# A decoder's four FFNs on one core: a new order at their seams, and the key/value product moved behind the third FFN's first pair

## Chip, cores and metric

The kernel runs on 1 core of one Trainium2 chip. The metric is the device time of one execution in microseconds, the median of the runs. The host only lays data out.

## What is computed

One inference step of a two-layer decoder on 512 prompt tokens and 64 sample tokens (8 sequences of 8), all in float32. Each layer has an FFN, a mixer and another FFN; the mixer of the first layer is a recurrent block, that of the second is windowed attention. All attention reads one key and value product, computed from the stream x between the second and the third FFN.

```python
def rms_norm(x, g):
    y = x * lax.rsqrt(jnp.mean(x * x, axis=-1, keepdims=True) + EPS)
    return y * g

def swiglu(x, w_gu, w_down):
    gu = x @ w_gu
    return (jax.nn.silu(gu[..., :D_FF]) * gu[..., D_FF:]) @ w_down

for l in range(DEPTH):                                   # DEPTH = 2
    x = x + 0.5 * swiglu(rms_norm(x, ffn1_norm[l]), ffn1_w_gu[l], ffn1_w_down[l])
    hn = rms_norm(x, mix_norm[l])
    x = x + (recurrent_block(hn, ...) if l < N_A else window_attention(hn @ w_q, k, v, ...) @ w_o)
    x = x + 0.5 * swiglu(rms_norm(x, ffn2_norm[l]), ffn2_w_gu[l], ffn2_w_down[l])
    if l == N_A - 1:
        kv = rms_norm(x, kv_norm) @ w_kv                 # 1024 x 256
y = rms_norm(x, final_norm)
```

D_MODEL is 1024 (8 tiles of 128 rows), D_FF 2816 (22 inner tiles).

## The kernel before

Everything is kept transposed: x is 8 tiles of 128 features by 576 tokens, in two halves of 288 columns. Every float32 operand of a matrix product is split into a rounded part (ACT, `_hi`) and a remainder (DVE, `_lo`, line 1266), and each product is three matmuls: high by high, high by low, low by high (`mm_k`, line 529; `product`, line 560).

The kernel is one program per engine, each an order written out by hand; engines meet only at semaphores, and an engine that waits holds up all that stands behind it in its own order. SP issues the weight loads.

**FFN.** The up product (gate and up weights of one inner tile, called a pair, index `g`) uses a two-by-two Strassen scheme with seven products P1 to P7 over blocks of x (B11, B12, B21, B22 and sums T1 to T4) and of weights (A11, A12, A22 and sums X1 to X4). Each product is 12 matmuls (4 tiles of x by 3), so a pair has 84. `pair` (line 608) orders them on PE: A11, then A22 of the pair before (`p4`, line 570), A12, X1, and X2, X3, X4 (`p637`, line 575). Between them ACT snaps partial results out of PSUM (S1, S5, S2, S7: `s1` at line 955, `s5` 970, `s2` 972, `s7` 935), DVE adds them up, applies 1/rms to the gate, ACT does silu, DVE multiplies by the up half. The loop body on ACT and on DVE is called `window` (lines 947 and 1338). The 22 pairs of an FFN come in chunks of 8, 8 and 6; after a chunk, 8 down products (`job`, line 539) of 8, 8 or 6 inner tiles add into x. The down product is multiplied by 1/rms and -0.5 in PSUM (line 1377) and then added (line 1380).

The norm is not applied to x ahead of the product: x is multiplied by the gain only; 1/rms comes from a matmul of ones with the sum of the squares (`stats`, line 627), a square root on ACT (`root`, line 1034) and a reciprocal on DVE (`invert`, line 1429), and is applied to results.

**Seams.** Before the second and the fourth FFN, `mixer_out` (lines 1039 and 1434) takes the eight output products one by one: DVE updates x, ACT multiplies by the gain (line 1002), and after each second product a tile of all seven blocks of x is made, rounded in two groups of 3 and 4 blocks (lines 1008 and 1013), its remainders taken by DVE (line 1404). `first_pair` (line 585) then goes tile by tile: A11, A12 and X1 for one tile, then for the next; the square sum follows, and X2, X3, X4. Silu of the first pair waits for 1/rms; in `window` it stands on ACT between the S1 snapshot and the rounding of A22.

The second FFN is followed by the key/value product: its last down products split x times the key/value gain (`split_x`, lines 1015 and 1412), two products of 48 matmuls each follow (`key_value` on PE, line 731, with the square sum inside the first), and ACT and DVE have their own `key_value` (lines 1194 and 1593) that make the third FFN's blocks of x, 1/rms (line 1599), the scaled keys (1604) and values (1612). The key/value weights use the `raw` buffers as all others do; the third FFN's first pair is loaded (line 461) once the last of these is split. `turn_values` (line 643) transposes the values in the third FFN's second pair.

## Time and profile before

| | us |
|---|---|
| median of 3 runs | 2044.31 (2042.05 to 2045.15) |
| the profiled execution | 2043.77 |
| its span, first to last instruction | 2042.0 |
| PE busy in the span | 1959.9 |
| DVE busy | 1505.9 |
| ACT busy | 964.0 |
| mean granted TensorE clock | 0.989 of 2.4 GHz |

Times in all rows are us from the span's start. PE runs matmuls; PEld loads weights and overlaps it; DVE, ACT and POOL are the vector, scalar and GpSimd engines. A line such as `L1266` is the program line that issued the instruction; helpers have one line for many uses, so the names `out<-in` tell them apart: `gw` are the split weights of a pair, `w_hi` and `w_lo` those of other products, `xs_hi` and `xs_lo` the split blocks of x, `act_hi` and `act_lo` the inner tiles, `temp` the scratch of a pair or the blocks of x before they are split, `raw` the landed weights.

### The profile page before, as it was taken

What the parts mean: (1) busy time and instruction counts of PE and PEld (TensorE: products, weight loads), DVE (VectorE), ACT (ScalarE), POOL (GpSimd) and SP (SyncE); (2) the same over time, 40 slices, a digit from 0 to 9 for tenths busy, and PEclk for the clock granted to TensorE, in tenths of its full rate; (3) what the DMA queues carried; (4) which work ended last, traced back from release to release, by engine and by line L of the source; (5) the groups of instructions that cost most, each with busy time, mean ns of one, the idle gap of its engine ahead of it and who ended that gap; (6) DMA issues with size and microseconds to landing.
All of it is one profiled execution on the core that took longest, in us unless ns stands there. A gap on an engine that the chain in (4) does not pass through costs nothing.

```text
span 2042.0 us, 34956 instructions
## 1 busy us (share of the span) xinstructions
PE 1959.9 (96%) x14465; PEld 1933.5 (95%) x14465; DVE 1505.9 (74%) x2111; ACT 964.0 (47%) x1490; POOL 58.1 (3%) x82
## 2 busy tenths in 40 slices
PE   4999999999998999999979999999999999999996
PEld 4999999999998999999979999999988999999996
DVE  5966957788778858758689578587575787586676
ACT  5543534437755525425465245254365554253352
POOL 0000000002200000000000000000010000000001
PEclk9999999999999999999989999999999999999998
DMA  3231222222221322322222223223200122222221
GB/s 134 84 104 64 103 88 99 79 90 81 83 86 62 110 77 83 104 83 79 81 74 103 84 83 107 80 83 123 83 32 1 63 84 104 82 93 94 83 88 62
DMA packets 55151, 172.69 MB, mean 85 GB/s; under 512 B 6320, under 2 KB 12752, under 8 KB 54976
## 3 DMA queue, kind: packets, MB, share of 16 engines
q1 hardware_dynamic: 53200, 166.09, 23.4%
q0 software_dynamic: 784, 3.04, 0.4%
q8 instruction: 115, 1.88, 0.4%
q10 hardware_dynamic: 1008, 1.31, 0.2%
q14 instruction: 44, 0.36, 0.1%
HBM read 167.72 MB, written 3.69 MB: 84 GB/s over the span
## 4 chain that ended last, share of the span: by engine, by line
PE 87%; DVE 7%; ACT 3%; issue 2%; DMA 1%; DVEq 0%; SPq 0%; ACTq 0%
PE ps L564 46%; PE ps L535 37%; PE ps L758 1%; PE ps L783 1%; DVE rstd L1431 1%; DMA raw<-w_gu 1%; DVE xs_lo L1266 1%; PE ps L768 1%; DVE gw L1266 1%; PE ps L639 0%; ACT xs_hi L1013 0%; PE ps L863 0%; DVE gw_f L1501 0%; DVE raw L1296 0%; DVE x L1753 0%
## 5 line engine op out<-in xcount | busy, mean ns | idle before, releaser
L564 PE MATMUL ps<-xs_hi,gw 128*128 128x288 f32 x4928 | 1004.8, 297 | 55.7 <-DVE gw L1266 23.7
L564 PEld LDWEIGHTS ps<-xs_hi,gw 128*128 128x128 f32 x4928 | 801.9, 190 | 61.2 <-DVE gw L1266 24.3
L564 PE MATMUL ps<-xs_lo,gw 128*128 128x288 f32 x2464 | 731.8, 297 | 0.0
L564 PEld LDWEIGHTS ps<-xs_lo,gw 128*128 128x128 f32 x2464 | 467.3, 190 | 0.2
L1266 DVE TENSOR_TENSOR gw<-raw,gw 128x1024 fp32r<-128x1024 f32 x352 | 383.2, 1091 | 83.1 <-ACT gw L923 33.4
L535 PE MATMUL ps<-act_hi,w_hi 128*128 128x288 f32 x1632 | 349.4, 296 | 0.4 <-DVE w_lo L1266 0.4
L535 PE MATMUL ps<-act_lo,w_hi 128*128 128x288 f32 x1632 | 349.5, 296 | 0.0
L535 PE MATMUL ps<-act_hi,w_lo 128*128 128x288 f32 x1632 | 349.3, 296 | 0.0
L901 ACT ACTIVATE w_hi<-raw 128x1024 fp32r<-128x1024 f32 (+1 forms) x142 | 143.5, 1010 | 366.9 <-PE ps L535 361.4
L535 PEld LDWEIGHTS ps<-act_hi,w_hi 128*128 128x128 f32 x1632 | 262.8, 189 | 0.6 <-issue 0.6
L535 PEld LDWEIGHTS ps<-act_lo,w_hi 128*128 128x128 f32 x1632 | 263.0, 189 | 0.0
L535 PEld LDWEIGHTS ps<-act_hi,w_lo 128*128 128x128 f32 x1632 | 263.0, 189 | 0.0
L1377 DVE SCALAR_TENSOR_TENSOR ps<-ps,rstd 128x576 f32<-128x576 f32 x96 | 73.6, 767 | 238.5 <-PE ps L535 238.5
L1266 DVE TENSOR_TENSOR w_lo<-raw,w_hi 128x1024 fp32r<-128x1024 f32 (+1 forms) x142 | 166.7, 1174 | 46.5 <-ACT w_hi L901 46.0
L923 ACT ACTIVATE gw<-raw 128x1024 fp32r<-128x1024 f32 x88 | 93.5, 1062 | 75.9 <-DVE raw L1303 71.6
L912 ACT ACTIVATE gw<-raw 128x1024 fp32r<-128x1024 f32 x88 | 93.3, 1060 | 74.9 <-PE ps L564 65.2
L1296 DVE TENSOR_TENSOR raw<-raw 128x1024 f32<-128x1024 f32 x88 | 107.3, 1219 | 3.8 <-DMA raw<-w_gu 3.8
L535 PE MATMUL ps<-xs_hi,w_hi 128*128 128x256 f32 (+2 forms) x480 | 104.3, 299 | 3.1 <-ACT gw_f L1099 3.1
L535 PE MATMUL ps<-xs_lo,w_hi 128*128 128x256 f32 (+2 forms) x480 | 103.3, 297 | 0.0
L535 PE MATMUL ps<-xs_hi,w_lo 128*128 128x256 f32 (+2 forms) x480 | 103.0, 296 | 0.0
L935 ACT ACTIVATE temp<-ps 128x288 f32<-128x288 f32 x88 | 36.2, 412 | 135.6 <-PE ps L564 135.6
L929 ACT ACTIVATE gw<-raw 128x1024 fp32r<-128x1024 f32 x88 | 92.5, 1051 | 0.0
(204 smaller groups left out, 1964.5 us busy)
## 6 DMA issues: line engine op xcount, KB each, us to landing
raw<-w_gu SPq DMA_DIRECT2D x176, 512.0 KB, 4.0
raw<-w_dn SPq DMA_DIRECT2D x32, 512.0 KB, 3.6
raw<-w_dn SPq DMA_DIRECT2D x32, 384.0 KB, 3.3
raw<-w_dn SPq DMA_DIRECT2D x32, 320.0 KB, 3.1
raw<-w_rec SPq DMA_DIRECT2D x20, 512.0 KB, 3.3
raw<-w_dn SPq DMA_DIRECT2D x32, 192.0 KB, 2.4
raw<-w_out SPq DMA_DIRECT2D x8, 512.0 KB, 3.3
raw<-w_q SPq DMA_DIRECT2D x8, 512.0 KB, 3.3
```

What stands on the lines that cost most here:

```text
L535: ins = nc.tensor.matmul(ps[:, 2 * slot + c, 0:width], wv(a, w, kw), halves(b, o, width), start=first and n == 0, stop=last and n == 2)
L564: ins = nc.tensor.matmul(ps[:, bank, 0:HT], gv(wt, w)[:, 0, p * P:(p + 1) * P], xb(xt, p, b)[:, 0, :], start=start and i == n == 0, stop=s ...
L758: ins = nc.tensor.matmul(ps[:, b0 + b // 2, c:c + hi - lo], q, kdup[p:p + 64, g, lo:hi], start=True, stop=True)
L768: ins = nc.tensor.transpose(ps[:, 6 + t // 4, (t % 4) * P:(t % 4 + 1) * P], prob[h % 2][:, (t + 1) * P:(t + 2) * P], ident[:, :])
L901: nc.scalar.activation(w_hi[:, c % 2, 0:KT[c] * P], std_raw(c), ACT.Copy).then_inc(hi_made, 1)
L912: nc.scalar.activation(gv(g_hi, A11, 2), pair_raw(g, R_A11, 2), ACT.Copy).then_inc(a_hi_made, 1)
L923: nc.scalar.activation(gv(g_hi, X1, 2), pair_raw(g, R_X1, 2, 3), ACT.Copy).then_inc(x12_hi_made, 1)
L929: nc.scalar.activation(gv(g_hi, X4, 2), pair_raw(g, R_A21, 2, 3), ACT.Copy).then_inc(x43_hi_made, 1)
L935: nc.scalar.activation(s7, ps[:, bank_a(g), 0:HT], ACT.Copy).then_inc(snapv2_made, 1)
L1266: nc.vector.tensor_tensor(out, a, b, ALU.subtract).then_inc(made, 1)
L1296: nc.vector.tensor_tensor(pair_raw(g, R_X1, 2), pair_raw(g, R_A21).broadcast_to([P, 2, BW]), pair_raw(g, R_A22, 2), ALU.add).then_inc(x14_ ...
L1377: own(nc.vector.scalar_tensor_tensor(acc, acc, -0.5, two(rstd[:, :]), ALU.mult, ALU.mult))
```

## The change

1. **Blocks of x at the seams.** The seven blocks are laid out B11, T1, B21, B22, T3, T2, T4, and rounded and subtracted in three groups of 2, 2 and 3 blocks. The first group needs only the first of a tile's two products (`x_t1`). X1 and X4 of the first pair are summed one product earlier, the remainder of A11 and A12 comes after product 5 and that of X1 and X2 in product 6. The weights' split for the key/value products is done in this loop.
2. **First pair on PE.** In the second, third and fourth FFN: A11 for all four tiles, A12 for three, X1 for four, A12 for the last. In all four FFNs the square sum stands between X2 and X3, no longer ahead of X2.
3. **First two windows** of each FFN get their own order on ACT and DVE (`first_windows`): 1/rms comes later, and silu of the first pair stands behind the second pair's last snapshot.
4. **Key/value product.** The second FFN's last down products go through `mixer_out`, as the output products do, straight into the third FFN's blocks. The key/value operand is split after that, into the `act` buffers, and the two products come on PE behind the third FFN's first pair, in other PSUM banks. Their weights are loaded into the unused end of the `act` buffers during the second FFN's last chunk, ahead of the load of its third pair. `turn_values` moves to the third pair.
5. **1/rms of the second FFN's last chunk** multiplies each of the 6 inner tiles (in `hidden`) and not the 8 down products; one instruction then does x - 0.5 times the product.

```diff
-B11, B21, B22, T1, T3, T2, T4 = range(X_BLOCKS)
+B11, T1, B21, B22, T3, T2, T4 = range(X_BLOCKS)
@@ SP
+            if j in kv_jobs:
+                return (act_hi_f, act_lo_f)[j - base["kv"]][:, 6 * NT:6 * NT + D_MODEL]
...
-                    last = max(j for j in range(a, b) if slot_of[j] // 2 == g % 2)
+                    last = max(j for j in range(a, b) if slot_of[j] // 2 == g % 2 and j not in kv_jobs)
...
+                        if f == 1 and c == 2 and g == g0 + 1:
+                            sp.wait_ge(job_done, base["dn", 1, 1] + KD)
+                            for i, j in enumerate(kv_jobs):
+                                sp.dma_start(std_raw(j), A["w_kv"][i]).then_inc(kv_landed, 16)
@@ PE
-            def p637(g):
+            def p637(g, stat=None):
                 product(a, X2, T2, False, stop=False).then_inc(p6_done, 1)
+                if stat is not None:
+                    stats(stat)
                 pe.wait_ge(x43_lo_made, g + 1)
...
+                    for t in tiles:
+                        ins1 = p1(*t)
+                    for t in tiles[:3]:
+                        p2(*t)
+                    for t in tiles:
+                        ins5 = p5(*t)
+                    ins2 = p2(*tiles[3])
...
-                if stat is not None:
-                    stats(stat)
-                p637(g)
+                pe.wait_ge(cmb_ready, 12 * f + 12)
+                p637(g, stat)
...
             def key_value():
                 j = base["kv"]
-                slot_free(pe, j)
-                job(j, j % 2, KD, xs_tile, order=NORD, ready=lambda k: (xs_ready, KD + k + 1),
-                    inside=(2, lambda: stats(3)))
-                slot_free(pe, j + 1)
-                job(j + 1, (j + 1) % 2, KD, xs_tile, used=v_tile_used)
+                job(j, 2, KD, hid_tile, w=0, ready=lambda k: (xs_ready, KD + k + 1))
+                pe.wait_ge(std_made, 4)
+                job(j + 1, 3, KD, hid_tile, w=1)
@@ ACT
+            def first_windows(g, stat, c0):
+                hi_x43(g)
+                snap_1(g)
+                hi_a22(g)
+                hi_a(g + 1)
+                act.wait_ge(cmb_ready, 12 * (g // FT) + 12)
+                snap_5(g)
+                snap_v1(g)
+                if g == 2 * FT:
+                    for n in range(3):
+                        kv_hi(n)
+                root(stat)
+                if g == 2 * FT:
+                    for n in range(3, KD):
+                        kv_hi(n)
+                hi_x12(g + 1)
+                snap_v2(g)
+                hi_x43(g + 1)
+                snap_1(g + 1)
+                hi_a22(g + 1)
+                hi_a(g + 2)
+                snap_5(g + 1)
+                snap_v1(g + 1)
+                silu(g)
+                hid_hi(g, 0, c0)
+                hi_x12(g + 2)
...
+                    if f == 1 and last:
+                        mixer_out(c0, 2, stat_out)
+                        continue
...
                     x_scaled_to(f, i, x_temp, m % 2)
-                    if m % 2:
+                    if m % 2 == 0:
+                        square(m, stat)
                         x_hi_first(f, i)
-                    square(m, stat)
-                    if m % 2:
+                    else:
+                        x_hi_second(f, i)
+                        square(m, stat)
                         x_hi_rest(f, i)
+                    if m == 4:
+                        hi_a(FT * f)
+                    if m == 6:
+                        hi_x12(FT * f)
+                prep_next(j0 + KD - 1)
@@ DVE
             def hidden(g):
+                if FT + CHUNKS[2][0] <= g < 2 * FT:
+                    own(nc.vector.tensor_tensor(y, y, rstd[:, :], ALU.mult))
...
+            def first_windows(g, stat):
+                lo_x43(g)
+                lo_a22(g)
+                sum_x14(g + 1)
+                lo_a(g + 1)
+                if g == 2 * FT:
+                    keys()
+                sum_x23(g + 1)
+                lo_x12(g + 1)
+                gate_sum(g)
+                lo_x43(g + 1)
+                up_second(g)
+                if g == 2 * FT:
+                    values()
+                else:
+                    invert(stat)
+                gate_scaled(g)
+                lo_a(g + 2)
+                hidden(g)
+                lo_a22(g + 1)
+                sum_x14(g + 2)
+                hid_lo(g, 0)
+                sum_x23(g + 2)
+                lo_x12(g + 2)
...
+            def mixer_out(j0, f, stat, scale=1.0):
+                    nc.vector.scalar_tensor_tensor(two(x[:, n, :]), ps2(j % 2), scale, two(x[:, n, :]), ALU.mult,
+                                                   ALU.add).then_inc(dve_evac, 1)
+                    if m < KD - 1:
+                        prep_next(j)
                     if m == 6:
                         sum_x23(g)
+                    if m % 2 == 0:
+                        x_t1(f, m // 2)
+                        x_lo(f, m // 2, 0)
+                    else:
+                        x_sums(f, m // 2)
+                        x_lo(f, m // 2, 1)
+                        x_lo(f, m // 2, 2)
+                    if m == 5:
+                        lo_a(g)
+                    if m == 6:
                         lo_x12(g)
                     add_square(m, stat)
+                    if m == 4:
                         sum_x14(g)
+                prep_next(j0 + KD - 1)
...
+            def keys():
+                for n in range(KD):
+                    dve.wait_ge(xs_hi_made, KD + n + 1)
+                    nc.vector.scalar_tensor_tensor(act_tile(act_lo, n), x[:, n, :], params[:, MIX_GAIN[1], n:n + 1],
+                                                   act_tile(act_hi, n).bitcast(F32), ALU.mult,
+                                                   ALU.subtract).then_inc(xs_ready, 1)
+                invert(3)
```

## Rows read from the trace of the kernel before

**Rows 1.** The page, part 1: PE's busy us, share of the span, instructions.

```profile
PE 1959.9 (96%) x14465; PEld 1933.5 (95%) x14465; DVE 1505.9 (74%) x2111; ACT 964.0 (47%) x1490; POOL 58.1 (3%) x82
```

**Rows 2.** Windows: length; PE, PEld, DVE, ACT, POOL busy; PEclk, DMA share, GB/s.

```profile
606.00:646.00 40.00, 33.63 (x238) 31.92 (x237) 35.10 (x39) 22.97 (x32) 0.00 (x0) 1.00 0.19 69
...
660.00:704.00 44.00, 44.00 (x333) 44.00 (x332) 39.41 (x52) 25.64 (x40) 0.00 (x0) 1.00 0.27 96
...
1015.00:1064.00 49.00, 33.78 (x222) 32.61 (x221) 42.20 (x49) 29.25 (x38) 3.88 (x5) 0.83 0.19 69
```

**Rows 3.** PE's waits, 1010 to 1066 us: in total, times, longest.

```profile
PE ps L564 <- DVE xs_lo L1266: 9.9, 1, 9.9
PE ps L564 <- DVE ssum L1612: 3.6, 1, 3.6
PE ps L632 <- DVE ssum L1427: 1.8, 1, 1.8
```

**Rows 4.** Chain that ended last: start, us, what.

```profile
1018.29 4.78 DMA raw<-w_gu
...
1046.16 16.59 PE ps L564 x102
```

**Rows 5.** Timeline of PE after the 9.9 us wait: start, us, what.

```profile
1041.20 0.44 PE L564 MATMUL ps<-xs_lo,gw 128*128 128x288 f32 x1
1041.44 0.68 PE L564 MATMUL ps<-xs_hi,gw 128*128 128x288 f32 x2
```

**Rows 6.** PE's waits, 595 to 650 us, before the second FFN.

```profile
PE ps L564 <- ACT temp L970: 3.7, 2, 2.6
PE ps L564 <- DVE x L1440: 1.6, 1, 1.6
PE ps L564 <- DVE xs_lo L1266: 1.1, 2, 0.6
```

**Rows 7.** DVE's instruction groups, 560 to 1100 us: busy, mean ns, idle before.

```profile
L1266 DVE TENSOR_TENSOR gw<-raw,gw 128x1024 fp32r<-128x1024 f32 x82 | 100.4, 1224 | 20.6 <-ACT gw L923 10.2 <-ACT gw L929 6.0 <-ACT gw L912 4.4
...
L1303 DVE TENSOR_TENSOR raw<-raw 128x512 f32<-128x512 f32 x28 | 19.3, 688 | 0.7
...
L1427 DVE TENSOR_TENSOR ssum<-ssum,sq 128x576 f32<-128x576 f32 x14 | 10.5, 753 | 0.6 <-ACT sq L1031 0.6
...
L1266 DVE TENSOR_TENSOR w_lo<-raw,w_hi 128x768 fp32r<-128x768 f32 x8 | 7.6, 952 | 3.0 <-ACT w_hi L901 2.9
...
L1431 DVE RECIPROCAL rstd<-sq 128x576 f32<-128x576 f32 x2 | 7.5, 3746 | 0.0
...
L1416 DVE SCALAR_TENSOR_TENSOR xs_lo<-x,params_sb,xs_hi 128x576 fp32r<-128x576 f32 x8 | 6.5, 816 | 0.0
...
L1399 DVE SCALAR_TENSOR_TENSOR temp<-temp 128x288 f32<-128x288 f32 x5 | 2.3, 459 | 0.2
...
L1266 DVE TENSOR_TENSOR xs_lo<-act_hi_f,xs_hi 128x864 fp32r<-128x864 f32 x2 | 2.1, 1048 | 0.0
```

**Rows 8.** ACT's instruction groups, 560 to 1100 us.

```profile
L929 ACT ACTIVATE gw<-raw 128x1024 fp32r<-128x1024 f32 x27 | 28.4, 1051 | 0.0
...
L939 ACT ACTIVATE temp<-temp 128x576 f32<-128x576 f32 x26 | 17.7, 679 | 1.4 <-DVE temp L1320 1.3
...
L972 ACT ACTIVATE temp<-ps 128x288 f32<-128x288 f32 x26 | 10.7, 411 | 27.5 <-PE ps L564 27.5
...
L939 ACT ACT_TABLE_LOAD x2 | 2.6, 1283 | 0.0
```

**Rows 9.** Timeline of PE at the head: square sum, then X2.

```profile
34.52 9.61 PE L639 MATMUL ps<-act_hi_f,ones_sb 128*128 128x288 f32 x32
43.76 0.51 PE L564 MATMUL ps<-xs_hi,gw 128*128 128x288 f32 x1
```

**Rows 10.** Timeline of ACT at the head: the squares of x.

```profile
32.48 4.69 ACT L1233 ACTIVATE act_hi_f<-x 128x576 f32<-128x576 f32 x8
```

**Rows 11.** Timeline of DVE at the end of the second FFN's last pairs.

```profile
978.41 0.46 DVE L1332 TENSOR_TENSOR temp<-ps,temp 128x288 f32<-128x288 f32 x1 [1.56 <-PE ps L564]
```

More of the change, by code:

```diff
@@ L507, in _ @@
             ffn(1)
-            products(base["kv"], [A["w_kv"][i] for i in range(2)])
             ffn(2)
@@ L537, in mm_k, with job @@
                 return ins
-            def job(j, par, kt, operand, cut=EVEN, ready=None, inside=None, used=None, order=range(KD)):
+            def job(j, par, kt, operand, cut=EVEN, ready=None, inside=None, order=range(KD), w=None):
                 pe.wait_ge(lo_made, j + 1)
@@ L598, in first_pair @@
                         pe.wait_ge(x12_lo_made, g + 1)
-                    pe.wait_ge(cmb_ready, 8 * f + 2 * i + 2)
-                    ins5 = product(a + 2, X1, T1, i == 0, (p,), False)
+                    return product(a + 2, X1, T1, i == 0, (p,), False)
+                tiles = [(p, p) for p in range(N_PAIR)]
+                if f == 0:
+                    for i, p in tiles:
+                        ins1, ins2, ins5 = p1(i, p), p2(i, p), p5(i, p)
+                else:
[6 more added lines that the diff above has]
+                    ins2 = p2(*tiles[3])
                 ins1.then_inc(p1_done, 1)
@@ L980, in ffn @@
                     g0, g1, c0 = pairs_of(f, c)
-                    for g in range(g0, g1):
-                        window(g, g0, g1, c0, stat_in if c == 0 and g == g0 else None)
+                    if c == 0:
+                        first_windows(g0, stat_in, c0)
+                    for g in range(g0 + 2 * (c == 0), g1):
+                        window(g, g0, g1, c0)
                     snap_v2(g1 - 1)
@@ L1219, in _ @@
             act.wait_ge(params_loaded, 16)
[L1220 removed]
+            for i, p in enumerate(range(N_PAIR)):
                 if i == 3:
[L1222 removed]
+                    act.wait_ge(cmb_ready, 3)
                 for b in range(2):
@@ L1372, in ffn @@
                     last = c == len(CHUNKS) - 1
+                    if f == 1 and last:
+                        mixer_out(c0, 2, stat_out, -0.5)
+                        continue
                     for m in range(KD):
```

209 lines of the change are left out of this document (102 added, 107 removed).

## The prediction, made before the changed kernel was run

> **What bounds the kernel now.** First the page's busy times: PE is busy 1959.9 us of the span of 2042.0 [rows 1], so 82 us are all that a new order can win, and another engine's work counts only where PE waits for it. Second the windows [rows 2]: between seams (660 to 704) PE never idles, 333 matmuls in 44 us at clock 1.00, that is 0.132 us each and 1.6 us for a product of 12; around the key/value product (1015 to 1064) it is busy 33.8 of 49 us, at clock 0.83; before the second FFN it loses 6.4 of 40 us, at clock 1.00. Third, who ends PE's waits at the key/value seam [rows 3]: 9.9, 3.6 and 1.8 us, 15.3 together. The chain tells why: the third FFN's first weights are asked for only when the key/value weights are split, and take 4.78 us to land [rows 4]; then sums, 1/rms and remainders of all four x tiles follow on DVE. After the long gap the clock is at 1.2 GHz: matmuls start 0.24 us apart [rows 5], and 102 of them take 16.59 us [rows 4] where 13.5 would do. 3.1 us, and 0.7 for the six before, make 19 us lost at this seam. Before the second FFN the waits are 1.6, 1.1 and 3.7 us [rows 6]; the seam before the fourth repeats them, the second such.
>
> **The change, part by part.** E is the end of the last product ahead of a seam. Where DVE works without a pause an instruction takes 0.08 us less than its row, and a hand-over between engines costs 0.03 to 0.05.
>
> *Key/value seam, until the first pair is done.* A down product here has 6 inner tiles, 36 matmuls, 4.8 us. DVE now does per product (prices: [rows 7]): x update 0.75 (576 wide, as are the square's sum and the remainder of two blocks), weight remainder 0.95; for an even product T1 0.46, remainder 0.75, square 0.75; for an odd one three sums of 0.46, remainders of 0.75 and 1.05, square 0.75. With the waits for ACT's rounding between them that is 4.4 us (even) and 5.7 (odd): 10.1 against 9.6 for two products, so DVE falls behind. It begins product 4 some 1.1 us late, product 5 1.6 (X1 and X4, 1.22 like every instruction 1024 wide, were added), product 6 3.3 (remainder of A11 and A12), and product 7's x update starts 5.7 us after E, because product 6 also brings the key weights' remainder, two sums of 0.69 and the remainder of X1 and X2. PE therefore does A11 on three tiles (1.2 us), waits 2.4 for tile 3's first blocks, works 1.6, waits 1.1 for the x update at E+6.5, works 1.6, waits 1.1 for tile 3's second blocks (9.2) and 2.1 for the snapshot S1 (11.7), which on ACT stands behind the value weights' rounding and that of X4 and X3, 1.05 each [rows 8]. Sum 6.7 us. Then products X2, the square sum, X3 and X4 run through; the first pair ends at E+17.7. Loading is off this path: the pair's weights are now released when product 5's weights are split, some 14 us earlier.
>
> *The key/value product behind it.* Its 96 matmuls (12.7 us) are done before and after; what matters is what hides behind them. ACT rounds the first x tile at E+13.8, DVE subtracts (0.82 each) from 16.3, so the operand is there at 17.1 and PE asks at 17.7; the last tile is there at 22.1, asked for at 23.3. The reciprocal (3.75 in the row), the key evacuation and the next pair's splits end near E+30.3, PE leaves the value product at 30.5 and needs them at 35. I cost this at nothing; without this cover the reciprocal's 3.7 us would be bare. Bounds: a gain is excluded, the work being the same; 3 us if the eight subtractions slip behind.
>
> *The third pair of every FFN.* This is a new wait. In the new first windows ACT does silu of pair 0 only after the last snapshot of pair 1, with a table load of 1.28 before it [rows 8]. From the end of pair 1's X2 product: snapshot 0.45, load and silu 2.0, two hidden products 0.9, A22's remainder 0.6, X1 and X4 of pair 2 1.15, hidden remainder 0.7, X2 0.7, ACT's rounding of X1 and X2 1.05, snapshot S7 0.4, in all about 8.0 with hand-overs. PE has X3, X4 and the next pair's A11 left, 4.8 us, of which the wait for the hidden tile eats 0.2; then A22 needs S7. So 3.0 us idle, in each of the four FFNs. The old order had silu inside pair 1 and no such wait. Bounds: 0, if something pulls the load ahead, and 3.7, what the old order lost in the same place [rows 6].
>
> The row of the table load starts as soon as ACT is free and is followed at once by its function; nothing beside the 1.28 us shows. The Trainium skill ("ScalarE: Activation LUTs", section "What ACT_TABLE_LOAD costs") adds a drain of about 1380 ns to each switch of the set. By that rule each of the four waits would be 4.4 and the total 5.5 us later than mine; the trace does not bear it out.
>
> *Seams of the second and fourth FFN.* A product here takes 6.4 us, DVE needs 4.9 and 6.2, so it keeps up until product 5 (remainder of A11 and A12) and begins product 7 0.5 us late, where before it was 1.6 late and PE waited. With A11 on all tiles first, A12's last tile after X1, PE waits only 0.8 for S1. So 6.4 becomes 0.8 + 3.0: 2.6 saved at each seam. Bounds: 0 and 6.4.
>
> *Head.* Before, PE did the 32 matmuls of the square sum (9.2 us from their start to X2's [rows 9]) while ACT squared x (4.7 us [rows 10]) and made S1. Now X2 comes ahead of the sum, and S1 stands behind ACT's eight squares: PE waits from 33 to 37.3, then does X2 and the whole sum. X3 starts at 37.3 + 1.6 + 9.2 = 48.2; before, X2 at 43.8, 1.6 and a wait of 1.1 as in [rows 6] made 46.6: 1.6 later. The wait of 2.6 in the second pair goes, here too, and 3.0 come in the third: 2.0 lost. Bounds: 0.7 saved (both old waits gone, only the third pair's 3.0 come) and 6 lost (the clock falls in the gap of 4.4).
>
> *1/rms on the last inner tiles.* Six multiplications of 0.76 more, eight passes over the product fewer; the first lie in windows where DVE is busy 39.4 of 44 us [rows 2]: 9.9 of a pair's 11.1, 10.7 with them. At the last pair DVE stood 1.56 us waiting for A22 [rows 11], which takes the 0.8. Nothing; bounds 0 and 2. The key/value weights' two loads stand on SP before a pair load that waits anyway until A22 of the pair two before is split: nothing.
>
> **Sum.** Key/value seam 19 - 6.7 - 3.0 = 9.3 saved; second and fourth FFN 2 x 2.6; head 2.0 lost: 12.5. The profiled execution took 2043.8 (span 2042.0 and 1.8 around), 0.5 under the median; from the median 2044.3 I forecast 2031.8.
>
> **The rivals.**
> 1. *The third pair's waits do not come* (the load or S7 gets through earlier): 4 x 3.0 more saved, 2019.8. For it: a load has no operand to wait for. Against: it stands behind ACT's snapshot in program order, and in the rows it starts where its line stands. 0.13.
> 2. *DVE's queue reaches further*: each even product 0.4 longer than my sum makes product 7 start nearly 2 us later, the key operands come 1 late, and the wider gaps bring the clock to 1.2 GHz in one first pair, 3.8 as it cost before. 6.8 less saved: 2038.6. For it: the 10.1 against 9.6; against: the rows before kept such chains to 0.03 us. 0.22.
> 3. *Slower*: the clock falls at each of the four new waits of 3 us and in the head's 4.4. A fall cost 3.8 here [rows 4, 5]; five are 19, so 2050.8. It decides whether an idle of 3 us suffices: 2.6 did not [rows 2, 6], 9.9 did. 0.05. The Trainium skill ("TensorE: Matmul & The Clock Gate", section "HAM oscillation — how this bites in real kernels") has idle between bursts of matmuls bring the clock back to half; by it this is the way the order would lose.
> 4. *The change does not do what it says*: PE reaches the key product without operands and the gap of 9.9 [rows 3] only moves there: 2041.7. 0.05.
>
> **How the numbers follow.** Forecast 0.55 (its own range 2027 to 2036), the rivals 0.13, 0.22, 0.05 and 0.05. The low end 2019 takes in rival 1, the high end 2040 rival 2; outside lie rivals 3 and 4, 1 in 10, and the tails of 1 and 2, about as much. A measurement of this kernel tells 0.2% (4.1 us) from no change. Faster: forecast, rival 1 and nearly all of 2, 0.88. Same: rival 4 and the rest of 2, 0.07. Slower: 0.05.
>
> **What would show it.** Right: PE's waits at the key/value seam near 2.4, 1.1, 1.1, 2.1 and none in the key and value products; in every FFN one wait near 3 us at the third pair's A22 product, ended by the ACT snapshot behind X1's rounding; X3 of the head at 48. Wrong: a clock under 0.9 in the key/value seam, a wait on the key operands, DVE waits in the second FFN's last six pairs that reach PE, or third pairs without a wait.

## The result, and the profile after

The changed kernel takes **2031.36 us** (median of 5 runs, 2029.91 to 2032.33) against 2042.05 for the kernel before, run beside it; the ratio is 0.9941 with a 95% interval of 0.9931 to 0.9952 (the two medians alone give 0.9948). Forecast were 2031.8 us, in a range of 2019 to 2040. The profiled execution took 2031.4 us, with a span of 2029.6 where the kernel before had 2042.0: 12.4 us less.

The total is right partly by luck: one term (the head) was 1.6 too small, and another (the fourth FFN's seam) 1.0 the other way. Besides, the forecast counts from a median of 2044.3; against the 2042.05 measured beside it, the medians differ by 10.7 us, not 12.5. The page's busy times (columns as in [rows 1]) show that TensorE's work did not change: as many matmuls, 2.4 us less busy time. The other 10.0 us of the span are waiting that went (82.1 us of TensorE's idle time became 72.1):

```profile
PE 1957.5 (96%) x14465; PEld 1933.2 (95%) x14465; DVE 1501.8 (74%) x2141; ACT 967.3 (48%) x1506; POOL 58.1 (3%) x82
```

**By stage.** The first down product of each FFN is easy to find in the timeline of PE (the first instruction of the down products' line after the FFN's weights' line). Its start, and the distance from one FFN to the next, cut the run into five stages. All kernels below are set against "after" in this table, us:

| kernel | start to 1st FFN | 1st to 2nd | 2nd to 3rd (key/value) | 3rd to 4th | rest | span |
|---|---|---|---|---|---|---|
| before | 132.92 | 583.18 | 420.55 | 586.80 | 318.55 | 2042.0 |
| after | 136.51 | 580.29 | 411.12 | 583.19 | 318.49 | 2029.6 |
| forecast for after | +2.0 | -2.6 | -9.3 | -2.6 | 0 | -12.5 |
| measured | +3.6 | -2.9 | -9.4 | -3.6 | -0.1 | -12.4 |

A single stage carries some noise: in four kernels below that change nothing in the head (the runs on the 1/rms, the order on TensorE, the key/value splits and the split in parts), the first column is 135.1 to 135.9.

**Key/value seam.** PE's waits from 1010 to 1066 us; the first line and the third belong to the third FFN's first pair, the other two to its third pair:

```profile
PE ps L569 <- DVE xs_lo L1338: 2.9, 2, 2.5
PE ps L569 <- ACT temp L965: 2.6, 1, 2.6
PE ps L569 <- ACT temp L981: 1.9, 1, 1.9
PE ps L569 <- DVE temp L1409: 0.3, 1, 0.3
```

Against [rows 3] the 9.9, 3.6 and 1.8 are gone. In the timeline of PE the last product ends where the first pair starts, at 1015.6; the waits stand in brackets, and the key product (L542) follows the first pair without one:

```profile
1019.46 0.40 PE L569 MATMUL ps<-xs_hi,gw 128*128 128x288 f32 x1 [2.47 <-DVE xs_lo L1338]
...
1020.52 0.69 PE L569 MATMUL ps<-xs_hi,gw 128*128 128x288 f32 x2
1021.24 0.69 PE L569 MATMUL ps<-xs_hi,gw 128*128 128x288 f32 x2
...
1024.92 0.41 PE L569 MATMUL ps<-xs_hi,gw 128*128 128x288 f32 x1 [0.40 <-DVE xs_lo L1338]
...
1027.48 0.37 PE L569 MATMUL ps<-xs_hi,gw 128*128 128x288 f32 x1 [1.90 <-ACT temp L981]
...
1033.31 0.42 PE L542 MATMUL ps<-act_hi,w_hi 128*128 128x288 f32 x2
```

The key product starts at E+17.7, as forecast (E, the end of the last product, is 1015.6). On the way there, though, PE waited 4.8 us, not 6.7, and was slow for the rest: from 1020.52 to 1021.24 three matmuls start, 0.24 us apart as in [rows 5], where 0.13 is the full pace. The window 1019 to 1023 below has a granted clock of 0.60. DVE's queue came as forecast. Its updates of x for the last two products, from the timeline of DVE:

```profile
1014.26 0.75 DVE L1558 SCALAR_TENSOR_TENSOR x<-ps,x 128x576 f32<-128x576 f32 x1
...
1021.40 0.75 DVE L1558 SCALAR_TENSOR_TENSOR x<-ps,x 128x576 f32<-128x576 f32 x1
```

The last one starts 5.8 us after E (forecast 5.7).

**Third pair.** From the timelines of ACT, DVE and PE in the second FFN: the last snapshot of the second pair, the table load, silu of the first pair; then (on DVE, not shown) the hidden tile and the sums; the rounding of the third pair's X1 and X2, the snapshot S7, and PE's A22 product, which waited for it:

```profile
641.89 0.41 ACT L991 ACTIVATE temp<-ps 128x288 f32<-128x288 f32 x1 [1.19 <-PE ps L569]
642.32 1.28 ACT L969 ACT_TABLE_LOAD   x1
643.61 0.69 ACT L969 ACTIVATE temp<-temp 128x576 f32<-128x576 f32 x1
...
648.19 1.06 ACT L953 ACTIVATE gw<-raw 128x1024 fp32r<-128x1024 f32 x1 [2.32 <-DVE raw L1375]
649.16 0.39 ACT L965 ACTIVATE temp<-ps 128x288 f32<-128x288 f32 x1
```

```profile
645.30 0.37 PE L569 MATMUL ps<-xs_hi,gw 128*128 128x288 f32 x1 [0.27 <-DVE temp L1409]
649.69 0.37 PE L569 MATMUL ps<-xs_hi,gw 128*128 128x288 f32 x1 [2.56 <-ACT temp L965]
```

2.56 for S7 and 0.27 for the hidden tile, in all four FFNs alike (2.57 and 2.58 in the first and third): the new wait, forecast at 3.0, is there.

**Head.** Timeline of PE in the first FFN's first pair: X2 after its wait for S1, the square sum, X3:

```profile
38.29 0.58 PE L569 MATMUL ps<-xs_hi,gw 128*128 128x288 f32 x1 [4.47 <-ACT temp L981]
...
41.30 9.08 PE L667 MATMUL ps<-act_hi_f,ones_sb 128*128 128x288 f32 x32
50.00 0.51 PE L569 MATMUL ps<-xs_hi,gw 128*128 128x288 f32 x1
```

X3 starts at 50.0, forecast 48.2. X2 itself took 3.0 us for 12 matmuls, not 1.6.

**Granted clock** (windows, columns as in [rows 2]; the clock is the number after POOL's), around the second FFN's first pair, in the stretch between seams, and behind four waits:

```profile
606.00:646.00 40.00, 38.87 (x287) 38.26 (x286) 34.45 (x43) 24.70 (x34) 0.00 (x0) 1.00 0.15 53
660.00:704.00 44.00, 44.00 (x332) 44.00 (x331) 39.82 (x52) 25.45 (x40) 0.00 (x0) 1.00 0.27 96
...
37.00:42.00 5.00, 3.71 (x14) 3.60 (x15) 4.10 (x4) 3.34 (x7) 0.00 (x0) 0.50 0.26 82
649.00:656.00 7.00, 6.31 (x36) 6.34 (x37) 6.58 (x9) 4.44 (x8) 0.00 (x0) 0.76 0.10 37
1019.00:1023.00 4.00, 3.54 (x15) 3.39 (x16) 2.97 (x5) 1.34 (x3) 0.00 (x0) 0.60 0.00 0
1641.00:1649.00 8.00, 5.44 (x30) 5.23 (x29) 7.43 (x12) 3.92 (x6) 0.00 (x0) 0.79 0.36 131
```

0.50 is the lower level, 1.2 GHz, for the whole window. The first window is the one of [rows 2]: 33.63 us busy of 40 became 38.87. The two are not quite alike, though: the kernel before has its wait of 2.56 us inside that window (it ends at 644.20), the changed kernel has its own behind it (647.13 to 649.69). The first FFN's third pair shows the fall too: 0.79 from 70 to 78 us, behind the 2.57.

### The profile page after: what moved, and what is told of

Its sections match the earlier page's. It is cut to its first block, busy times and chain, and to the rows that moved or that the text cites. A ratio compares the mean times of both kernels' runs of the same rounds, so it can differ in the third digit from the quotient of the medians.

```text
span 2029.6 us, 35039 instructions
## 1 busy us (share of the span) xinstructions
PE 1957.5 (96%) x14465; PEld 1933.2 (95%) x14465; DVE 1501.8 (74%) x2141; ACT 967.3 (48%) x1506; POOL 58.1 (3%) x82
## 4 chain that ended last, share of the span: by engine, by line
PE 89%; DVE 5%; ACT 3%; issue 2%; DMA 1%; DVEq 0%; SPq 0%; ACTq 0%
PE ps L569 47%; PE ps L542 37%; PE ps L786 1%; PE ps L811 1%; PE ps L796 1%; ACT xs_hi L1088 1%; DMA raw<-w_gu 1%; DVE gw L1338 0%; PE ps L667 0%; PE ps L891 0%; DVE gw_f L1627 0%; DVE x L1558 0%; DVE x L1877 0%; ACT w_hi L931 0%; ACT temp L1083 0%
## 5 line engine op out<-in xcount | busy, mean ns | idle before, releaser
L1338 DVE TENSOR_TENSOR gw<-raw,gw 128x1024 fp32r<-128x1024 f32 (+1 forms) x352 | 383.0, 1091 | 78.5 <-ACT gw L953 40.9
L542 PE MATMUL ps<-act_hi,w_hi 128*128 128x288 f32 x1664 | 356.1, 296 | 0.0
L542 PE MATMUL ps<-act_lo,w_hi 128*128 128x288 f32 x1664 | 356.0, 296 | 0.0
L542 PE MATMUL ps<-act_hi,w_lo 128*128 128x288 f32 x1664 | 355.8, 295 | 0.0
L542 PEld LDWEIGHTS ps<-act_lo,w_hi 128*128 128x128 f32 x1664 | 268.0, 189 | 0.0
L542 PEld LDWEIGHTS ps<-act_hi,w_lo 128*128 128x128 f32 x1664 | 268.0, 189 | 0.0
L542 PEld LDWEIGHTS ps<-act_hi,w_hi 128*128 128x128 f32 x1664 | 267.9, 189 | 0.0
L1486 DVE SCALAR_TENSOR_TENSOR ps<-ps,rstd 128x576 f32<-128x576 f32 x88 | 67.5, 767 | 230.6 <-PE ps L542 230.6
L542 PE MATMUL ps<-xs_hi,w_hi 128*128 128x256 f32 (+2 forms) x448 | 97.9, 301 | 3.1 <-ACT gw_f L1191 3.1
L542 PE MATMUL ps<-xs_lo,w_hi 128*128 128x256 f32 (+2 forms) x448 | 96.9, 298 | 0.0
L542 PE MATMUL ps<-xs_hi,w_lo 128*128 128x256 f32 (+2 forms) x448 | 96.9, 298 | 0.0
```

The costliest lines, as they stand in the source:

```text
L542: ins = nc.tensor.matmul(ps[:, 2 * slot + c, 0:width], wv(a, w, kw), halves(b, o, width), start=first and n == 0, stop=last and n == 2)
L1338: nc.vector.tensor_tensor(out, a, b, ALU.subtract).then_inc(made, 1)
L1486: own(nc.vector.scalar_tensor_tensor(acc, acc, -0.5, two(rstd[:, :]), ALU.mult, ALU.mult))
```

## The experiments

Each is the changed kernel with one edit, timed beside the kernel before. Ratios are to that one; the intervals reach 0.0008 to 0.0014 to either side, so between two kernels here some 3 to 4 us can be told apart by times, and less only by the trace. Stages come from one profiled execution of each kernel, up to 2.5 us from the median of its runs.

### The head's order undone

```diff
+                if stat == 0:
+                    stats(stat)
                 pe.wait_ge(snap1_made, g + 1)
                 product(a, X2, T2, False, stop=False).then_inc(p6_done, 1)
-                if stat is not None:
+                if stat:
                     stats(stat)
```

> The first FFN alone gets its old order back: the square sums ahead of X2. My theory of the head's loss (3.6 us by the traces, not the 2.0 forecast): X2 ahead of the sums waits 4.47 us for S1 behind ACT's eight squares (38.29), and the clock granted in that gap falls to 0.55, so X2 takes 3.0 us, not 1.6. With the sums back in that place, their own pace fills the stretch, X3 starts near 47 us, not at 50.00, the clock stays up there, and the run is 2.5 to 3.5 us faster than the changed kernel: about 2028.3. Rival (what is late in FFN 1 is the third pair, and the head is hidden behind it): X3 early but the first down product at 136.7 as now, 0 us.

2023.11 us, ratio 0.9908 [0.9895, 0.9922], span 2020.0: about 8 us faster, more than twice what I expected. By stage, the start to the first FFN is 127.98 instead of 136.51; the others are within 0.9. Of these 8.5, 7.0 come from the head, up to the start of X3. The rest is the clock behind the third pair's wait, 1.00 from 62 to 70 us where the changed kernel has 0.79 (70 to 78); the edit does not touch that place. Timeline of PE in that run:

```profile
33.73 8.03 PE L669 MATMUL ps<-act_hi_f,ones_sb 128*128 128x288 f32 x32
41.38 0.51 PE L569 MATMUL ps<-xs_hi,gw 128*128 128x288 f32 x1
```

and its clock:

```profile
35.00:40.00 5.00, 5.00 (x22) 3.90 (x21) 2.10 (x3) 4.92 (x9) 0.00 (x0) 1.00 0.00 0
40.00:45.00 5.00, 5.00 (x34) 4.63 (x33) 3.38 (x4) 1.59 (x2) 0.00 (x0) 1.00 0.59 213
```

The sum follows the first pair without a gap, at clock 1.00, and takes 7.65 us (33.73 to 41.38), where in [rows 9] it took 9.24, with 0.69 granted from 35 to 40 us, and in the changed kernel 8.70. X2 has no wait, since ACT made S1 meanwhile; X3 follows at about 43.0, 7 us ahead of the changed kernel's. So moving X2 ahead of the sum costs this kernel not 2 us but some 7. Against the kernel before it looks like 3.6 only because that kernel lost time in the same place too: its X3 started at 46.83, after a sum 1.6 us longer, a wait of 1.10 us ahead of X3 and a start 0.8 later. Why its clock fell there is not shown: TensorE's order is the same, and in all four kernels here that put the first FFN's sum first the clock stayed at 1.00 in the head.

### S7 ahead of the rounding of X1 and X2

```diff
                 hid_hi(g, 0, c0)
+                snap_v2(g + 1)
                 hi_x12(g + 2)
...
-                if g > g0:
+                if g > g0 and (g - g0 != 2 or g0 % FT):
                     snap_v2(g - 1)
                 hi_x43(g)
```

> In the third pair of every FFN, ACT takes the snapshot S7 ahead of the rounding of X1 and X2 of that pair. My theory: the wait of 2.57 us for S7 (four times) is one of order on ACT alone, S7's sum is ready long before; the A22 product then starts 2.5 us earlier, and of what comes next the X1 product waits at most 0.3 us for its weights. The four waits fall to 0.3 or less each, the dips of the clock to 0.76 to 0.79 behind two of them go as well: 9 to 12 us faster than the changed kernel, about 2021. Rival (another wait takes the place): the X1 product of the third pair, whose weights hang on the same chain of silu, hidden and the sums X2 and X3, waits instead for 1.5 to 2.5 us; then 0 to 4 us faster, 2029.

2024.72 us, 0.9912 [0.9899, 0.9926]: 6 to 7 us faster, between the expectation and its rival. The waits for S7 are gone, and the clock stays at 1.00 in the second and fourth FFN (windows 640 to 655 and 1640 to 1655). By stage, 2.6, 1.6 and 2.0 are gained in the first, second and fourth FFN and nothing in the third, where the first pair's clock was 0.82 in this execution (1011 to 1030; 0.91 from 1015 to 1034 in the changed kernel). PE's waits over the whole run show what came instead, four waits for the snapshot S5 (the second line; the first is S1, as it was):

```profile
PE ps L569 <- ACT temp L981: 8.2, 4, 4.5
PE ps L569 <- ACT temp L987: 6.1, 4, 1.5
```

Not X1 waits (0.24 us) but X3, two products on, for S5, which ACT takes behind the rounding of the second pair's hidden tile. The order of ACT was the cause of the 2.57, and the next late link of the same chain took 1.5 of it.

### The table load moved out of the chain

```diff
                 root(stat)
+                nc.scalar.activation(tab[:, :], eps[:, :], ACT.Silu)
```

> A silu of one column, whose result nobody reads, stands right behind each FFN's square root on ACT, so that the table for silu is loaded there and not between pair 1's last snapshot and its silu. My theory: the load of 1.28 us is a link of the chain silu, hidden, sums X2 and X3, rounding, S7 that the third pair waits for, and taking it out shortens each of the four waits from 2.57 to about 1.3 us: 5 us faster than the changed kernel, 2026. Rival (the rule cited in the prediction, which would put about 2.7 us on each load): the waits go altogether, 10 us faster, 2021. Second rival (the load is moved to where something else waits, the second pair's X1 weights): 0 us.

2027.3 us, 0.9921 [0.9908, 0.9935], 4 us faster. The load now stands behind the square root. In the first FFN, timeline of ACT (last snapshot of the second pair, silu of the first):

```profile
61.40 0.41 ACT L992 ACTIVATE temp<-ps 128x288 f32<-128x288 f32 x1 [1.19 <-PE ps L570]
61.70 0.68 ACT L970 ACTIVATE temp<-temp 128x576 f32<-128x576 f32 x1
```

From one start to the other 0.30 us instead of 1.72: the load is worth 1.42. The Trainium skill ("ScalarE: Activation LUTs", section "What ACT_TABLE_LOAD costs") adds a drain of about 1380 ns to each switch; nothing of that size came free here, so the rule does not hold in this place. In the first and third FFN the wait falls to 1.6 (expected 1.3) and the 0.27 goes. In the second and fourth it falls to 2.3 only: there silu waits for the scaled gate, which stands behind the reciprocal on DVE (638.69 in that run's timeline, 3.74 us of reciprocal ahead of it). Behind the 2.3 the clock stays at 1.00 in the second FFN (645 to 653) and falls in the fourth (0.79 from 1640 to 1648). The stages gain 3.1 and 2.2 in the first and second FFN and nothing in the third and fourth.

### 1/rms back on the eight products

```diff
-                if FT + CHUNKS[2][0] <= g < 2 * FT:
-
-                    own(nc.vector.tensor_tensor(y, y, rstd[:, :], ALU.mult))
...
+                    if f == 2:
+                        acc = ps2(j % 2)
+                        own(nc.vector.scalar_tensor_tensor(acc, acc, scale, two(rstd[:, :]), ALU.mult, ALU.mult))
+                        nc.vector.tensor_tensor(two(x[:, n, :]), acc, two(x[:, n, :]), ALU.add).then_inc(dve_evac, 1)
```

> The 1/rms goes back onto the second FFN's last eight products (one more DVE operation of about 0.8 us in each, in the scratch bank), and off the six inner tiles. My theory: DVE is already 5.6 us behind at the last product (its update at 1021.40 against a product that ends at 1015.8), so each of the eight multiplies lands on its queue, less what the first two products leave idle: the last update 5 to 6.5 us later, and the key/value seam with it: 2036 to 2038. Rival (the forecast's price of nothing for this part taken the other way, the multiplies lie beside PE): 0 us, 2031.

2037.84 us, 0.9974 [0.9965, 0.9982]: the theory's 6.5. The second to third FFN takes 418.15, 7.0 more, and no other stage moves by over 0.7. Timeline of DVE, the multiply and the update for the last product:

```profile
1025.43 0.76 DVE L1557 SCALAR_TENSOR_TENSOR ps<-ps,rstd 128x576 f32<-128x576 f32 x1
1026.22 0.76 DVE L1558 TENSOR_TENSOR x<-ps,x 128x576 f32<-128x576 f32 x1
```

The update comes 4.8 us later than in the changed kernel. Around the seam PE waits 2.1 us for weights' remainders, for which it did not wait there, and 1.4 at the start of the first pair, for which the trace names no releaser. The first pair itself then takes 20.6 us for 17.7; its waits are only 0.4 longer, the rest goes with the clock (0.78 from 1019 to 1042). So the part that I priced at nothing in its own place is worth 7 us at the seam, some 2.5 of them by the clock (an estimate, 20.6 - 17.7 - 0.4), since it takes eight operations off the queue that ends it.

### TensorE's order in the first pair undone

```diff
-                if f == 0:
+                if True:
                     for i, p in tiles:
                         ins1, ins2, ins5 = p1(i, p), p2(i, p), p5(i, p)
```

> TensorE alone takes the first pair of the second to fourth FFN tile by tile again (A11, A12, X1 of each), with ACT's, DVE's and the rest's new order kept. My theory: in the second and fourth FFN the end of the first pair hangs on ACT's queue (rounding of the last tile, the rounding of X3 and X4, then S1 at 627.33), which the order on TensorE does not touch; 0 to 0.3 us in each. In the third FFN X1 of the first tile waits about 4.4 us for its weights (split at 1019.59 to 1020.8), but the last tile and S1 come when they come now: 0 to 1.5 us by the clock. In sum 0 to 2 us slower, about 2032. Rival (the order on TensorE is what the second and fourth seams' gain comes from): 2.6 us lost in each of these and as much in the third: 2037 to 2039.

2031.82 us, 0.9949 [0.9936, 0.9961]: no difference. The third FFN's first pair has one wait of 5.6 us for the last update in place of 2.5, 0.4 and 1.9, and ends 0.1 us later (E+17.75). That stage is 1.6 longer, but behind the third pair's wait, where the clock is 0.79 (1061 to 1069) and was 1.00 in the changed kernel. The second and fourth FFN wait 0.5 and 0.8 in the first pair; from its start to the first down product both take as long as in the changed kernel (94.8 and 94.9 us). What is done first on TensorE hardly matters; the last operand does.

### Tile pairs split in one piece again

```diff
                     if m % 2 == 0:
                         square(m, stat)
-                        x_hi_first(f, i)
                     else:
+                        x_hi_first(f, i)
                         x_hi_second(f, i)
...
-                    if m % 2 == 0:
-                        x_t1(f, m // 2)
-                        x_lo(f, m // 2, 0)
-                    else:
+                    if m % 2:
+                        x_t1(f, m // 2)
                         x_sums(f, m // 2)
+                        x_lo(f, m // 2, 0)
```

> Before the second to fourth FFN, a tile pair's first part (B11 and T1) is rounded and split only with its second half again, as in the kernel before, so that three roundings and all the sums stand behind the last product's update; TensorE's order and all the rest stay new. My theory: the gain at these seams is this split: behind the last update ACT then has one more rounding (0.69 us) and DVE one more difference (0.45) and one more low part (0.76) ahead of what the first pair ends on: 1.3 to 1.9 us more waiting in each of three seams, 2035 to 2037. Rival (what gains is the weights' splits and the square sums being out of the way, and the split of a pair in two parts hides beside the last product anyway): 0 to 1 us, 2031 to 2032.

2039.75 us, 0.9985 [0.9976, 0.9993]: 8 us slower, by the ratios three quarters of what the change had gained (0.0044 of 0.0059). The stages lose 3.9, 2.2 and 3.4. PE's one wait in the second FFN's first pair, and the clock behind it:

```profile
625.85 0.61 PE L569 MATMUL ps<-xs_hi,gw 128*128 128x288 f32 x1 [2.79 <-DVE xs_lo L1338]
```

```profile
620.00:640.00 20.00, 17.21 (x115) 16.76 (x114) 16.17 (x22) 12.08 (x18) 0.00 (x0) 0.91 0.14 54
```

2.8 us in place of 0.86 is the upper end of what was expected; the clock, 1.00 there in the changed kernel, takes 1.5 more (from the first pair's start to the first down product the second FFN takes 3.4 us longer, the fourth 3.3). (In the third FFN 6.6 us stand in place of 4.8.) So the gain of the three seams hangs on two things about the end of DVE's and ACT's queues: this split, and, in the third, the eight multiplies.

### The square sum ahead of X2 in all four FFNs

```diff
+                if stat is not None:
+                    stats(stat)
                 pe.wait_ge(snap1_made, g + 1)
                 product(a, X2, T2, False, stop=False).then_inc(p6_done, 1)
-                if stat is not None:
-                    stats(stat)
```

> The square sum stands ahead of X2 again in the first pair of all four FFNs. From the run of the head alone (8.3 us faster) this differs by the second to fourth FFN. My theory: there the sum needs DVE's last addition of squares (ending at 628.2 in the second FFN), which comes 0.5 us after S1, so X2 starts some 1.0 us later and X3 about 0.5 later in the second and fourth; in the third the sum fits into the wait for S1 and gains 0.5: in all 0.5 us behind the run of the head, 2023.6. Rival (the old 1.6 us wait of the sum's place comes back in each): 4 to 5 us behind it, 2028.

2027.07 us, 0.9927 [0.9913, 0.994], against 0.9908 for the head alone; the intervals overlap. The median lies nearer the rival's 2028 than the theory's 2023.6; the profiled execution (2024.6) is the fastest of five, and its trace bears out the theory. By stage it is 0.3 and 0.5 behind in the second and fourth FFN, as the theory has it (waits of 1.4 for the last addition of squares come for those of 0.9 and 1.0 for S1), but 2.1 in the third, where it expected a gain. There a wait of 1.5 us takes the place of 1.9 for S1, and the key product does start 0.4 earlier (E+17.3). The loss comes behind it: 1.0 in the key and value products, which now wait 0.4 for an operand (the other 0.6 has no row), and 1.5 at the third pair, where the clock is 0.79 and was 1.00 in the run of the head. In the second and fourth FFN the new place of X2 is right by a small amount; in the first it is wrong.

### S1 ahead of X3 and X4, and the key/value splits later

```diff
-                hi_x43(g)
-                snap_1(g)
+                snap_1(g)
+                hi_x43(g)
                 hi_a22(g)
```

> In the first pair of every FFN, ACT takes the snapshot S1 ahead of the rounding of X3 and X4 (1.05 us). My theory: the waits for S1 (4.47, 0.86, 1.90 and 1.00 us) shrink by up to that, until the X3 product's weights are what comes last: 1.0 in the head, 0.6 each in the second and fourth FFN, 0.3 in the third, where the low parts of X3 and X4 come right behind: 2 to 3 us faster, 2029. Rival (X3's weights are late by as much, 0.4 us of S1 ahead of them): 0 to 1 us faster.

2029.5 us, 0.9932 [0.9919, 0.9944]: 2 us faster by the median, which times of this spread do not settle. The trace shows the mechanism and its limit. In the head the wait falls from 4.47 to 3.53. In the second and fourth FFN the wait for S1 is replaced by one of 0.6 for the last tile's low part. Their stages gained nothing; from the first pair's start to the first down product they gained 0.2 and 0.4.

```diff
                 if g == 2 * FT:
+                    snap_1(g)
+                    hi_x43(g)
+                    prep(base["kv"])
+                    prep(base["kv"] + 1)
...
-                sum_x14(g + 1)
-                lo_a(g + 1)
                 if g == 2 * FT:
-                    keys()
+                    keys(g + 1)
```

> The key/value weights' two splits (1.04 us each on ACT, 1.22 on DVE) move from between the last products' updates of the second FFN to behind S1 and the low parts of X3 and X4 in the third FFN's first pair, and the next pair's sum X1/X4 and low parts behind the eight low parts for the key product. My theory: DVE's queue decides when the first pair can go on; its update of the last product comes 1.2 us earlier, S1 no longer waits behind a split, so the waits of 2.47, 0.40 and 1.90 us lose about 2 in sum: 2029 to 2030. Rival (the work ahead of the key product is only reordered and its operands come when they come now, DVE having no idle time from 1008 to 1033): 0 us, with a new wait ahead of the key product.

2030.57 us, 0.9939 [0.9925, 0.9953]: no difference by times. (The edit also takes S1 ahead of X3 and X4 in the third FFN.) The waits of the first pair went from 4.8 to 3.8, half of what was expected, and the stage from 411.12 to 410.44. The rival's new wait ahead of the key product did not come either.

### The two that paid, together, and all of them

The first takes the head's order and S7's place from above, and in the third pair also:

```diff
                 snap_5(g + 1)
+                silu(g)
                 snap_v1(g + 1)
-                silu(g)
                 hid_hi(g, 0, c0)
...
+                early = g - g0 == 2 and g0 % FT == 0
+                if early:
+                    snap_5(g)
                 if g > g0:
                     hid_hi(g - 1, g - 1 - g0, c0)
-                snap_5(g)
+                if not early:
+                    snap_5(g)
```

> The first FFN's square sums ahead of X2 again (as in the run of the head), and in every third pair: S7 ahead of the rounding of X1 and X2 as in the run before, silu of pair 1 ahead of the last snapshot of pair 2, S5 of the third pair ahead of the rounding of the hidden tile. The run with S7 alone showed the X3 product waiting 1.54 us for S5 in its place. My theory: that wait hangs on the order of ACT (S5 behind the rounding of pair 2's hidden tile) and on silu's place, and falls under 0.4; so of 2.84 us in each of four third pairs about 2.4 go for good: 8.3 + 9.6 us and the two dips of the clock: 2012 to 2014. Rival (the two runs add up and the rest is taken by another wait): 2016 to 2017.

**2011.53 us**, 0.9843 [0.9829, 0.9856]: 20 us faster than the changed kernel and 32 than the kernel before, and slightly better than forecast. Stages: 125.77, 577.18, 410.06 and 579.54. PE's waits from 600 to 665 us, which were 2.6, 0.9 and 0.3:

```profile
PE ps L569 <- ACT temp L983: 0.9, 1, 0.9
PE ps L569 <- ACT temp L967: 0.5, 1, 0.5
PE ps L569 <- ACT temp L989: 0.3, 1, 0.3
```

The second kernel adds the table load's place, S1's and the key/value splits':

> All that gained so far in one kernel: the first FFN's square sums ahead of X2, the third pair's new order on ACT, the early silu table, S1 ahead of X3 and X4 in every first pair, and the key/value weights' splits behind them. My theory: what the run with both (2011.5) still waits for in the third pairs (0.5 for S7, 0.3 for S5, three times) hangs on silu with its table load and goes with it, some 2 us; S1 ahead brings 0.8 in the second and fourth FFN together, the key/value order 0.9: 2007.5 to 2009. Rival (these waits hang on the reciprocal ahead of the gate's scaling, not on the load): 2010 to 2011.

2012.97 us, 0.9854 [0.984, 0.9867], not to be told from the other, and 2 us above the rival's range. The rival's mechanism is what the trace shows. Timeline of ACT in the second FFN: S5 of the second pair, then silu of the first, which with its table long loaded waits for DVE's scaling of the gate, behind the reciprocal:

```profile
630.57 0.41 ACT L990 ACTIVATE temp<-ps 128x288 f32<-128x288 f32 x1 [0.48 <-PE ps L570]
632.86 0.69 ACT L972 ACTIVATE temp<-temp 128x576 f32<-128x576 f32 x1 [1.89 <-DVE temp L1410]
```

## Why the prediction was right, and where it was not

**Key/value seam: right, with two errors that cancel.** Forecast 9.3, measured 9.4. DVE's lateness, S1's place, the product's start at E+17.7 and no wait for its operands are as worked out, and the third pair's 2.85 stand for the 3.0. The step "PE waits 2.4, 1.1, 1.1 and 2.1" failed in part: 2.47, none, 0.40 and 1.90 came, and what was missing went into a clock of 0.60 behind the first of them. The run with the table load moved, which leaves this stretch as it was, shows the step without that fall (the clock stays at 1.00 from 1014 to 1023 there):

```profile
1014.10 0.40 PE L570 MATMUL ps<-xs_hi,gw 128*128 128x288 f32 x1 [2.45 <-DVE xs_lo L1340]
...
1016.85 0.40 PE L570 MATMUL ps<-xs_hi,gw 128*128 128x288 f32 x1 [0.90 <-DVE x L1560]
...
1019.56 0.40 PE L570 MATMUL ps<-xs_hi,gw 128*128 128x288 f32 x1 [0.85 <-DVE xs_lo L1340]
...
1022.12 0.37 PE L570 MATMUL ps<-xs_hi,gw 128*128 128x288 f32 x1 [1.90 <-ACT temp L982]
```

These are the four waits forecast, from the same releasers. Its clock falls only behind them (0.91 over 1010 to 1030), and the key product starts at E+19.3. So that E+17.7 came out is luck in part: the fall lay where PE would have waited anyway. I had put the clock's fall into a rival instead (2, "the wider gaps bring the clock to 1.2 GHz in one first pair"); it came without DVE being any later than my sum.

**The step that failed: "2.6 did not".** Rival 3 held that an idle of 2.6 us had left the clock alone in the kernel before, from [rows 2, 6]. The two windows that I read there end at 646 and begin at 660. The one between them, of the kernel before, says otherwise:

```profile
646.00:660.00 14.00, 14.00 (x96) 14.00 (x96) 12.71 (x18) 7.46 (x11) 0.00 (x0) 0.89 0.28 108
```

The kernel before already paid for its 2.56 us wait with the clock. The first and fourth FFN show the same (0.79 from 61 to 69, 0.89 from 1653 to 1667). The changed kernel keeps that wait and its dip (0.88 from 646 to 660) some 5 us later. So in these three FFNs rival 3's price was right in kind, but was no addition, and the run did not become slower. A fall behind these waits also costs less than its 3.8: some 1.5 us (the last section).

**Second and fourth FFN: right in mechanism, 0.3 and 1.0 too small.** Waits of 0.86 or 1.00, 0.27 and 2.56 against the forecast 0.8 and 3.0: 3.7 and 3.8 for 3.8. From the last product's end to the first down product the two seams save 3.7 and 3.5. 2.7 of this are listed waits; the remaining 0.9 has no row that I can name. In the second FFN's stage 0.8 went again before the seam, in a stretch without a changed line, where the runs above vary by 1.4. A wait for weights there is as long as before (2.43 us, ending at 551.31, and 2.41, ending at 554.78), but only the changed kernel's clock falls behind it. Windows of the kernel before and of the changed one:

```profile
551.00:559.00 8.00, 7.69 (x57) 7.69 (x58) 3.08 (x4) 7.27 (x11) 2.97 (x2) 1.00 0.31 105
```

```profile
554.00:562.00 8.00, 7.22 (x42) 7.22 (x43) 3.28 (x5) 6.49 (x10) 2.97 (x2) 0.79 0.20 66
```

That the seam's gain comes from the split, and not from TensorE's order as my text had it ("With A11 on all tiles first, A12's last tile after X1"), the two runs on these show: of the 3.7 and 3.5, 0.0 go with the order, 3.4 and 3.3 with the split.

**Head: the term that was mis-sized.** Forecast 2.0 lost, within bounds of 0.7 saved and 6 lost; measured 3.6 against the kernel before. The wait for S1 came as worked out (38.29, forecast 37.3). Left out of the sum, and put into its bound of 6 only, was the clock behind it: 0.50 from 37 to 42 us, X2 at 3.0 us for 1.6. And I took the square sum's 9.2 us of [rows 9] for its price. It is 7.65 at the full clock, as the run with the old order showed. So the right comparison for this edit is 7 us, not 3.6.

**Third pair: right.** 2.83 to 2.85 us in each of the four (2.56 to 2.58 of them at A22), forecast 3.0, by the chain that the prediction lists; the run with S7 alone took the A22 wait away and left 1.5 for S5, and the run with the table load shortened it by that link. Rival 1 (they do not come) is out. What I did not say is that a few moved lines in ACT's order bring it under 0.8, as the run with both shows.

**1/rms on the inner tiles: nothing, as forecast, on their side.** From 905 to 985 us PE has no wait. On the other side, at the key/value seam, undoing it costs 7 us, of the 9.4 gained there. No run undoes the move of the key/value product by itself, so its own share is not shown; the trace shows only that the 9.9, 3.6 and 1.8 us are gone.

**The Trainium skill's rule on idle gaps** ("TensorE: Matmul & The Clock Gate", section "HAM oscillation — how this bites in real kernels"), cited as the way in which the order would lose, agrees with the head: 4.47 us of idle, then the lower level. That the total came out all the same is due to the kernel before paying it too, behind waits in the first, second and fourth FFN.

## What to carry to other kernels

Read the granted clock right behind each wait, not in the windows beside it. A new order should be priced against the best order of the rest, not only against the kernel before: one edit of a bundle (here X2 ahead of the square sum) can cost 7 us and hide behind what the others gain, so undo the edits one at a time. At a seam, look first for what the last operand has behind the last update on the elementwise engines, since TensorE's own order is worth little until that is short.

## What the runs showed that I had not expected

The granted clock behind waits of nearly equal length differed: 0.76 and 0.79 behind 2.56 in the second and fourth FFN and 0.60 in the window behind 2.47 in the third, but 1.00 behind the third's 2.58 (1061 to 1068 us) and behind 1.54 with S7 alone. With the table load moved, a wait of 2.32 us left it at 1.00 in the second FFN and not in the fourth. It differs even behind the same wait of two kernels whose code is the same there, as at the third FFN's third pair in the run of the head and in the run with the sum ahead of X2 in all FFNs (2.56 us, ending at 1052.34, and 2.57, ending at 1053.12):

```profile
1052.00:1060.00 8.00, 7.66 (x58) 7.69 (x59) 7.86 (x11) 5.33 (x9) 0.00 (x0) 1.00 0.21 67
```

```profile
1053.00:1061.00 8.00, 7.88 (x49) 7.91 (x50) 7.86 (x11) 4.59 (x7) 0.00 (x0) 0.79 0.21 70
```

From the end of that wait to the first down product the first takes 66.14 us and the second 67.66: one such fall costs 1.5 us. The length of the wait alone does not tell whether it comes, and what does is not shown here; stages of single executions differ by such falls alone. What came of it can be as large as the waits: 1.9 us of new waiting in the second FFN, with the split undone, made its stage 3.9 us longer. And a sum of 32 matmuls that looked like a fixed price of 9.2 us was 7.65 at the full clock.
